# The second layer's query sums of squares: one set of two-column products on folded squares in place of two sets of one-column products

## The reference, cut to what matters

```
q = (rms_norm_2(cq, q_norm_g) @ w_q_up).reshape(b, s, A_HEADS, A_QK)     # 16 heads, A_QK = 128 + 64
...
q = rms_norm_2(q, q_gain)       # x * rsqrt(mean(x * x over 192) + 1e-6) * gain
...
q = jnp.concatenate([q[..., :A_NOPE], rope(q[..., A_NOPE:], pos)], axis=-1)
o = mla_attend(q, k, v, pos).reshape(b, s, A_WIDTH)
```

## Time and profile before

| | |
|---|---|
| Median of 3 runs | 3125.38 us (3125.1 to 3125.4) |
| Profiled execution, its own time | 3124.12 us |
| Its span, first to last instruction | 3122.3 us |
| TensorE busy | 3085.4 us, 99% of the span |
| VectorE, ScalarE, GpSimd busy | 1768.3, 1274.4 and 215.4 us |
| Granted TensorE clock, mean | 0.999 of full speed |

### The profile page before, as it was taken

The page is one execution under the profiler, slowest core; times in us unless marked ns, Lnnn a source line. Parts: engine busy times, 40 slices in busy tenths (PEclk is TensorE's granted clock), DMA queues, the critical chain, the costliest instruction groups (busy, mean ns, idle before and its releaser), DMA issues. The chain is left out here.

```text
span 3122.3 us, 51762 instructions
## 1 busy us (share of the span) xinstructions
PE 3085.4 (99%) x21393; PEld 2539.7 (81%) x21393; DVE 1768.3 (57%) x3073; ACT 1274.4 (41%) x2328; POOL 215.4 (7%) x170
## 2 busy tenths in 40 slices
PE   8999999999999999999999999999999999999999
PEld 6877777777778778788888888888888888888787
DVE  5335565656666754644457776335556656665822
ACT  4124343434434422524346665323344434443521
POOL 0000000001011101000111121110000000000000
PEclk9999999999999999999999999999999999999999
DMA  8433333342232353343331213534223323332452
GB/s 252 126 81 92 91 88 98 100 115 61 67 98 71 108 176 108 112 106 104 107 102 55 61 55 119 162 108 118 88 81 95 95 75 101 95 95 82 161 164 79
DMA packets 494639, 324.25 MB, mean 104 GB/s; under 512 B 27194, under 2 KB 449693, under 8 KB 494406
## 3 DMA queue, kind: packets, MB, share of 16 engines
q1 hardware_dynamic: 494374, 320.94, 35.1%
q10 hardware_dynamic: 32, 0.01, 0.0%
HBM read 276.05 MB, written 44.85 MB: 103 GB/s over the span
## 5 line engine op out<-in xcount | busy, mean ns | idle before, releaser
L550 DVE TENSOR_TENSOR WLT<-AR,WHT 128x1024 fp32r<-128x1024 f32 (+1 forms) x430 | 527.2, 1232 | 655.7 <-ACT WHT L544 654.9
L562 PE MATMUL PS<-XH,WHT 128*128 128x512 f32 (+1 forms) x2224 | 888.3, 399 | 2.7 <-DVE AR L1045 1.4
L564 PE MATMUL PS<-XH,WLT 128*128 128x512 f32 (+1 forms) x2224 | 867.5, 390 | 0.0
L544 ACT ACTIVATE WHT<-AR 128x1024 fp32r<-128x1024 f32 (+1 forms) x430 | 447.5, 1043 | 597.5 <-PE PS L564 464.1
L563 PE MATMUL PS<-XL,WHT 128*128 128x512 f32 (+1 forms) x1712 | 666.9, 390 | 0.0
L562 PEld LDWEIGHTS PS<-XH,WHT 128*128 128x128 f32 (+1 forms) x2224 | 416.3, 187 | 99.1 <-issue 9.3
L564 PEld LDWEIGHTS PS<-XH,WLT 128*128 128x128 f32 (+1 forms) x2224 | 416.0, 187 | 91.0
L563 PE MATMUL PS<-ARR,WHT 128*128 128x512 f32 x1024 | 398.6, 389 | 0.0
L563 PEld LDWEIGHTS PS<-XL,WHT 128*128 128x128 f32 (+1 forms) x1712 | 320.5, 187 | 66.0 <-issue 2.4
L563 PEld LDWEIGHTS PS<-ARR,WHT 128*128 128x128 f32 x1024 | 192.4, 188 | 39.4 <-issue 0.2
L562 PE MATMUL PS<-XL,WHT 128*128 128x512 f32 x512 | 199.7, 390 | 0.4 <-issue 0.4
(11 more groups left out here) (512 smaller groups left out, 5152.6 us busy)
## 6 DMA issues: line engine op xcount, KB each, us to landing
AR<-b_w_in SPq DMA_DIRECT2D x128, 512.0 KB, 4.0
AR<-w_in SPq DMA_DIRECT2D x122, 512.0 KB, 3.9
AR<-a_w_in SPq DMA_DIRECT2D x48, 512.0 KB, 4.6
AR<-w_out SPq DMA_DIRECT2D x32, 512.0 KB, 4.2
AR<-a_w_out SPq DMA_DIRECT2D x32, 512.0 KB, 3.9
AR<-b_w_out SPq DMA_DIRECT2D x32, 512.0 KB, 4.0
proj_scratch<-AR SPq DMA_DIRECT2D x33, 256.0 KB, 2.1
residual_scratch<-RES SPq DMA_DIRECT2D x8, 1024.0 KB, 6.1
```

The lines of the kernel that those rows point to most:

```text
L544: self.nc.scalar.activation(self.shaped(self.high, n), self.shaped(self.raw, n), ACT.Copy).then_inc(self.s_high, 1)
L550: self.nc.vector.tensor_tensor(self.shaped(self.low, n), self.shaped(self.raw, n), f32(self.shaped(self.high, n)), ALU.subtract).then_inc( ...
L562: mm(out, wh, xh[k0 + c], start=(start and c == 0), stop=False)
L564: last = mm(out, wl, xh[k0 + c], start=False, stop=(stop and c == nk - 1))
```

## The change

`query_square(i, e)` now squares each head's 128 features in two instructions of 64 partitions. The half that lies on head e's own partitions stays there and goes to `SQ[:, 0]`. The other half moves over to the same 64 partitions and goes to `SQ[:, 1]`. After both heads, `SQ[:, 0]` and `SQ[:, 1]` hold head 0's 128 squares folded on partitions 0 to 63, and head 1's on 64 to 127. GpSimd adds `SQ[:, 2]` and then `SQ[:, 1]` onto `SQ[:, 0]`, both on all 128 partitions and the second behind the first. So the first add now waits for the squares of both heads. TensorE then makes four products with two columns each: the moving operand is `cmask`, whose column e is one on the partitions of head e. The set for head 0 ahead of `values(i, 1)` is gone. VectorE reads the sums in another order.

```diff
-            def query_sums(i, e):
-                N.wait(pe, i, f"pool.sa{e}")
-                last = sums(SQ[:, e, :], (2 + e) * TB)
-                if e:
-                    N.did(last, "pe", "qns")
+            def query_sums(i):
+                N.wait(pe, i, "pool.sa1")
+                N.did(sums(SQ[:, 0, :], 2 * TB, 2), "pe", "qns")
...
-                          16: [lambda: query(0, 1)], 17: [lambda: query_sums(0, 0), lambda: query_sums(0, 1)],
+                          16: [lambda: query(0, 1)], 17: [lambda: query_sums(0)],
...
                     query(q, 1)
-                    query_sums(q, 0)
                     values(i, 1)
-                    query_sums(q, 1)
+                    query_sums(q)
                     scores(q, 0)
...
             def rotary_square(i):
                 N.wait(act, i, "dve.qg")
-                N.wait(act, i - 1, "pool.sa0", "pool.sa1")
+                N.wait(act, i - 1, "pool.sa1")
...
             def query_square(i, e):
-                N.wait(act, i, f"dve.cq{e}", f"pe.rk{e}")
-                N.did(A(SQ[:, e, :], FB[1 - e][:, :], ACT.Square), "act", f"sq{e}")
+                N.wait(act, i, f"dve.cq{e}", "pe.rk0", "pe.rk1")
+                A(SQ[rows(e), 0, :], FB[1 - e][rows(e), :], ACT.Square)
+                N.did(A(SQ[rows(e), 1, :], FB[1 - e][rows(1 - e), :], ACT.Square), "act", f"sq{e}")
...
-            def rotary_added(i, e):
-                N.wait(pool, i, "act.sqr", f"act.sq{e}")
-                x = SQ[rows(e), e, :]
-                N.did(Pt(x, x, SQ[rows(e), 2, :], ALU.add), "pool", f"sa{e}")
+            def squares_added(i):
+                N.wait(pool, i, "act.sqr", "act.sq0", "act.sq1")
+                N.did(Pt(SQ[:, 0, :], SQ[:, 0, :], SQ[:, 2, :], ALU.add), "pool", "sa0")
+                N.wait(pool, i, "pool.sa0")
+                N.did(Pt(SQ[:, 0, :], SQ[:, 0, :], SQ[:, 1, :], ALU.add), "pool", "sa1")
...
-                N.wait(pool, i, "pool.krl")
-                rotary_added(i, 0)
                 W.wait(pool, i, "act.qrh")
-                N.wait(pool, i, "pool.sa0")
                 W.did(Pt(QRL, QRF, f32(QRH), ALU.subtract), "pool", "qrl")
-                W.wait(pool, i, "pool.qrl")
-                rotary_added(i, 1)
-            N.wait(pool, NP - 1, "pool.sa1")
+                squares_added(i)
```

More of the change, by code:

```diff
@@ L3142, in _ @@
             for i in range(NP):
-                N.wait(pool, i - 1, "pool.sa1")
                 for e in heads:
@@ L3221, in query_factors @@
                 N.wait(dve, i, "pe.qns")
-                do("meanq", TS(RM[:, 2 * TB:4 * TB], MB[:, 2 * TB:4 * TB], 1.0 / QK, EPS, ALU.mult, ALU.add))
+                do("meanq", TS(RM[:, 2 * TB:4 * TB].rearrange("p (e b) -> p e b", e=2), MB[:, 2 * TB:4 * TB].rearrange("p (b e) -> p e b", e=2), 1.0 / QK, EPS, ALU.mult, ALU.add))
                 N.wait(dve, i, "act.rootq")
```

## The result

| | median, us | lowest to highest | profiled run, us | its span | granted clock |
|---|---|---|---|---|---|
| before | 3125.37 (6 runs) | 3124.67 to 3125.51 | 3124.12 | 3122.3 | 0.999 |
| changed | 3142.07 (6 runs) | 3139.98 to 3143.9 | 3143.9 | 3142.1 | 0.995 |

The changed kernel is slower: ratio 1.0053, 95% interval 1.004 to 1.0066, or 16.7 us of median against the 8.6 forecast. The time lies 1.1 us above the end of the range. The predicted chain is there nearly row by row, and beside it there is a lower clock that I had given 12%.

A forecast was written before the change was run, and what follows sets the result against it. TensorE, busy 99% of the span, was taken as the bound, so delays in the chain to its sums arrive in full. 6 x 1.08 + 1.50 + 0.62 = 8.6 us on 3125.38 gave 3134.0 us, range 3129.5 to 3141.0.

The forecast's parts named there:

- Half squares 0.61 apart, no cheaper than whole ones: ScalarE's squares in a turn: each second half adds 0.61 us, bounds 0.49 and 0.63, not half a price.
- VectorE's add back to 0.69, relief of 0.91 in the turns and 0.49 in turn 6: L3218, no longer beside head 0's GpSimd add, falls from 1.66 to 0.69 us; the following split starts earlier.
- Rival B: VectorE's add stays at 1.66 us because something else held it: 14.6 us slower, 3140.0 us; 5%.
- Values at 1633.33: Turn 0: TensorE's products with the values start after ScalarE's copies at about 1633.33 instead of 1633.72.
- Adds 1.35 apart, sums 1.08 us later, pause of 1.8: GpSimd's two adds run in sequence, so TensorE stands still 1.8 us instead of 0.33 ahead of the sums.
- Turn 6 at 1.50: Last preparation: ScalarE's split is twice as long, VectorE's split only 0.49 us earlier, so the turn loses 1.50 us.
- Pair 0 at 0.62: Between the tiles: L3218 already takes 0.69, nothing is won back, and the sums end 0.62 us later.
- The sum, 8.6 us: Whole kernel: six turns, turn 6 and pair 0 together, 6 x 1.08 + 1.50 + 0.62 us slower.
- Clock kept, 70%: Forecast case: TensorE's clock does not fall in the new pause, so only the 8.6 us with its bounds counts.
- the prediction's own step 2: Turn 0: products with the values wait for ScalarE's copies, run 3.33 us and are over at 1636.66.
- Rival A: TensorE's clock falls in the new pause, 1.4 us a fall; 3144 us if in all seven turns; 12%.
- Rivals C and D: Squares ready when the sums come, 3119.5 us, 5%; or half squares at half price, nearly nothing, 3128 us, 8%.

The follow-up runs named there:

- half a square less: Changed kernel without ScalarE's square of head 1's own half (64x512), that half missing from the sums: 3131.01 us, ratio 1.0017.
- The kernel before with a third add: Kernel before plus one GpSimd add of 128x512 behind head 1's add, for which the second sums wait; nothing folded: 3141.18 us, ratio 1.0048.
- one add less: Changed kernel with GpSimd's second add replaced by a copy of one column, folded halves left out of the sums: 3127.4 us, ratio 1.0005.
- Filling the pause: Changed kernel plus six thrown-away TensorE products of 128x512 between the products with the values and the sums: 3137.21 us, ratio 1.0035.
- the second profile: Profile of the changed kernel run once more with no edit, against the kernel before: 3140.9 us, ratio 1.0046.

## Why the prediction was wrong, step by step

- *Half squares 0.61 apart, no cheaper than whole ones*: right, 0.59 long and 0.61 apart in turn 0. The run with half a square less gives 0.53 us a turn back, so they are on the path.
- *VectorE's add back to 0.69, relief of 0.91 in the turns and 0.49 in turn 6*: right: 0.69 in all eight executions, and VectorE's split 0.86 earlier in turn 0 and 0.43 in turn 6. Rival B is out. The kernel before with a third add shows the other side: head 0's add stays beside it there (1637.35, 1.58 us long), and the same VectorE instruction, L3220 in that kernel, takes 1.66 again:

```profile
L3220 DVE TENSOR_TENSOR AR<-AR x8: 694/1662/1666, 1515.6 to 1909.9; 128x512 f32<-128x512 f32 x8
```
- *Values at 1633.33*: 0.2 early, without consequence for the chain. But the prediction counts the pause ahead of them as saved. It isn't: it was 0.69 of the loads' time ahead of head 0's sums and is 1.33 ahead of the values.
- *Adds 1.35 apart, sums 1.08 us later, pause of 1.8*: 1.35, 1.02 and 1.63. The run with one add less prices the second add at 1.05.
- *Turn 6 at 1.50*: 1.5.
- *Pair 0 at 0.62*: 1.4. What failed here is the 1.29 us for the second add: it took 2.12. I had written that the relief costs nothing elsewhere since behind L3218 only the split has two SBUF inputs and GpSimd is idle then. That holds in the turns. At pair 0 the split is two pieces of 128x1024 and runs from 1520.83 on, over the second add. Both slow down: 3.63 us for the two pieces of the split, where one took 1.21, and 0.86 more for the add. With no such add beside it the split takes 2.36 for both pieces. This bears on "SBUF — State Buffer", section "Who interferes with whom", of the Trainium skill, and agrees with its rule that a VectorE instruction with two SBUF inputs and a GpSimd instruction that reads SBUF contend. That only the later one stands still, as the prediction put it, the rows don't show: both last longer, and so did head 0's add before, 1.57 against 1.26, though it had started first. I had applied the rule only where it helped.
- *The sum, 8.6 us*: the chain costs 1.4 + 6.1 + 1.5 = 9.0. The mechanism and its size were right; of the 0.8 that pair 0 lacked, the six turns, 0.4 below their forecast, hide half.
- *Clock kept, 70%*: this is the step that failed and decided the outcome. The sum has nothing for the clock; the falls in the turns cost 4 x 1.5 = 6.0 us in one profiled execution and 3 x 1.5 = 4.5 in the other (1.4 each was forecast). I argued that one pause with long products on both sides would not do what two pauses with one-column products did. The premise was wrong: the turn has two pauses, 1.33 and 1.63 us, as the prediction's own step 2 implies, where TensorE's last query product is over at 1632.57 and the values start at 1633.33. The products behind the second are narrow ones. Rival A had the mechanism and the price, and it had 12%. Filling the pause removed all falls from the turns of the profiled execution; a longer pause in the kernel before brought some in. By what rule a given pause is followed by a fall stays open.
- *The range*: with three or four falls on the chain's 9.0 the kernel is at 3138.9 to 3140.4. What is missing to 3142.07 is not shown for the median, only for the profiled execution, at 3143.9 the slowest of the six: 4.7 us ahead of pair 0. A fall at pair 0, as in the second profile, can be part of it in others. Of the twelve profiled executions, of ten kernels, seven have one or two falls near 1070 and 1117, whatever was changed (that of the earlier trace rows is in all twelve). The 20 runs of the kernel before beside the first experiments reach from 3124.47 to 3130.44. A range worked out from the three runs shown, 0.3 us apart, had no room for that.
- Rivals C and D are excluded by the durations: 0.59 and 1.26 us, no shorter for fewer partitions.

## What to carry to other kernels

Work saved on the bounding engine is worth nothing when that engine then waits for a longer chain on slower engines: here 32 products (64 as the profile records them) and their loads were saved, and each turn lost 1.02 us, because a second GpSimd add and a second half square outweighed what VectorE's earlier split gave back. When a change opens a pause on TensorE like those of 1.4 to 2.5 us here, price a fall of the clock with it, as a chance per pause rather than as a yes or no, and look first for an order or an engine that closes the pause. A rule on a shared port must be applied at each place where the moved instruction will stand, and not only at the place where its departure helps.

## What the runs showed of the hardware that was not expected

- Whether the clock falls behind a pause differs between executions of the same program and between turns with the same pause: of 19 turns with pauses of 1.44 to 1.63 us ahead of the sums six had a fall, all three of 1.98 to 2.15 did, and none of the 50 of 0.29 to 1.11. None stands behind the 1.32 to 1.76 us ahead of the values either. At pair 0 pauses of 1.89 to 2.50 were followed by one in three of five profiles, that of 1.43 by none, and the single pause of 0.56, between two sets of eight one-column products, was too. So the pause's length alone does not decide.
- The same kind of fall happens in the first layer, near 1070 and 1117 us, in seven of twelve profiles: both in three of them, one in four. In the changed kernel's profile TensorE was busy 1.73 us of the 3 ahead of the first. Between 1065 and 1182 us the two made 3.9 us with what lies between, a scatter that no change made here touches.
- GpSimd's add of a tensor to itself takes 1.04 us for 128x512 (the kernel before with a third add), its add of two different tensors of the same size 1.26 or 1.27.
- VectorE's two-input instructions and GpSimd's slow each other down: 0.69 alone and 1.66 beside a GpSimd add for VectorE's add, 1.26 alone and 2.12 beside VectorE's split for GpSimd's.
- A square or an add takes as long on 64 partitions as on 128: ScalarE's square 0.59 against 0.60, GpSimd's add 1.26 against 1.27.
